# Gate and up as Strassen's seven block products, and a feed-forward in two phases

## The reference, cut to what matters

```python
x = _layernorm(ALPHA * x + g1 * o, ln1_g, ln1_b)
h = x * (1 + sc2) + sh2
gate, up = jnp.split(h @ w_gu, 2, axis=-1)      # 2048 -> 2 x 5632
f = (jax.nn.silu(gate) * up) @ w_down           # 5632 -> 2048
return _layernorm(ALPHA * x + g2 * f, ln2_g, ln2_b)
```

## Time and profile before

| what | value |
|---|---|
| runs, median (lowest, highest) | 3320.02 us (3313.26, 3322.87), 3 runs |
| span of the profiled execution | 3311.0 us |
| its own time beside the span | not given; the median of the runs is 9.0 us above the span |
| PE busy | 3168.8 us, 96% |
| DVE, ACT, POOL busy | 1653.1, 934.4, 207.6 us |
| moved by DMA | 341.86 MB, 103 GB/s |

### The profile page before, as it was taken

How to read it: one execution, slowest core, us unless ns; L and a number is a source line. 1 busy time by engine, 2 the same in 40 slices (tenths; PEclk the granted TensorE clock), 3 DMA queues, 4 the chain that set the end, 5 groups by cost and what they waited for, 6 DMA issues and landing times.

```text
span 3311.0 us, 44092 instructions
## 1 busy us (share of the span) xinstructions
PE 3168.8 (96%) x17294; PEld 2681.6 (81%) x17294; DVE 1653.1 (50%) x2086; ACT 934.4 (28%) x1393; POOL 207.6 (6%) x195
## 2 busy tenths in 40 slices
PE   7899999999999999899999999999999999999994
PEld 2687767777766678698989898989898999999983
DVE  7626665633333332556454535364545454545457
ACT  7425555533444311421211111111111111111121
POOL 0200010100000100062000000000000000000004
PEclk9999999999999999899999999999999999999997
DMA  9836655621200311132222222222222222222221
GB/s 369 275 126 206 196 192 190 206 93 52 108 32 32 123 65 64 45 91 82 71 77 71 77 77 77 74 73 77 72 76 77 77 72 76 77 71 77 77 96 64
DMA packets 91913, 341.86 MB, mean 103 GB/s; under 512 B 11878, under 2 KB 12090, under 8 KB 90714
## 3 DMA queue, kind: packets, MB, share of 16 engines
q1 hardware_dynamic: 82800, 302.55, 27.2%
q0 software_dynamic: 8224, 36.50, 3.4%
q10 hardware_dynamic: 730, 0.38, 0.0%
HBM read 327.42 MB, written 15.65 MB: 104 GB/s over the span
## 4 chain that ended last, share of the span: by engine, by line
PE 83%; DVE 8%; issue 3%; DMA 3%; ACT 2%; POOL 0%; DVEq 0%; ACTq 0%; SPq 0%; POOLq 0%
PE ps L1294 25%; PE ps L1296 25%; PE ps L1295 25%; PE ps L1465 2%; DVE wlo L927 1%; ACT whi L559 1%; DMA mraw<-in_wstream 1%; DVE acc L1278 1%; PE ps L1417 1%; DMA raw<-in_wstream 1%; PE ps L1416 1%; PE ps L1438 1%; DVE tmp L1245 1%; DVE mlo L942 1%; PE ps L1412 1%
## 5 line engine op out<-in xcount | busy, mean ns | idle before, releaser
L927 DVE TENSOR_TENSOR wlo<-raw,whi 128x1024 fp32r<-128x1024 f32 x497 | 617.2, 1249 | 1270.1 <-ACT whi L559 1265.1
L559 ACT ACTIVATE whi<-raw 128x1024 fp32r<-128x1024 f32 x497 | 519.3, 1058 | 1625.9 <-PE ps L1296 1602.5
L1294 PE MATMUL ps<-oh,whi 128*128 128x320 f32 x2816 | 872.3, 310 | 8.7 <-DVE tmp L1245 7.8
L1295 PE MATMUL ps<-ol,whi 128*128 128x320 f32 x2816 | 870.2, 309 | 0.0
L1296 PE MATMUL ps<-oh,wlo 128*128 128x320 f32 x2816 | 870.1, 309 | 0.0
L1294 PEld LDWEIGHTS ps<-oh,whi 128*128 128x128 f32 x2816 | 530.2, 188 | 12.5 <-DVE tmp L1245 11.2
L1295 PEld LDWEIGHTS ps<-ol,whi 128*128 128x128 f32 x2816 | 530.2, 188 | 0.1
L1296 PEld LDWEIGHTS ps<-oh,wlo 128*128 128x128 f32 x2816 | 530.0, 188 | 0.0
L1296 PE MATMUL ps<-whi,fl 128*128 128x512 f32 x820 | 327.0, 399 | 0.0
L1294 PE MATMUL ps<-whi,fh 128*128 128x512 f32 x820 | 322.4, 393 | 4.3 <-DVE wlo L927 3.7
L1295 PE MATMUL ps<-wlo,fh 128*128 128x512 f32 x820 | 323.2, 394 | 0.0
(11 more groups left out here) (251 smaller groups left out, 3831.0 us busy)
## 6 DMA issues: line engine op xcount, KB each, us to landing
raw<-in_wstream SPq DMA_DIRECT2D x503, 512.0 KB, 3.3
mraw<-in_wstream SPq DMA_DIRECT2D x64, 512.0 KB, 7.6
acc<-in_xT SPq DMA_DIRECT2D x8, 640.0 KB, 16.4
oscr<-ost POOLq DMA_DIRECT2D x16, 320.0 KB, 2.4
acc<-in_xtok POOLq DMA_DIRECT2D x1, 5120.0 KB, 16.3
ostage<-oscr POOLq DMA_DIRECT2D x16, 320.0 KB, 4.0
out_y<-acc POOLq DMA_DIRECT2D x5, 1024.0 KB, 4.2
tbl<-rpbpad POOLq DMA_DIRECT2D x16, 224.0 KB, 15.2
```

Source lines behind the costliest of these rows:

```text
L559: nc.scalar.activation(hi_of(n), raw[:, n % 4, :], ACT.Copy).then_inc(hi_ready, 1)
L927: V.tensor_tensor(lo_of(n), raw[:, n % 4, :], hi_of(n).bitcast(f32), ALU.subtract).then_inc(lo_ready, 1)
L1294: mm(out, ah, bh, start=first, stop=False)
L1295: mm(out, ah, bl, start=False, stop=False)
```

## The change

Gate and up are taken as one product of 2 x 2 blocks: the token halves (320 each), the halves of the contraction (1024 each), and gate and up (128 columns each per pair j, 44 pairs). Strassen's scheme (in Winograd's form) needs seven block products in place of eight, and sums of blocks before and after.

**Activations.** The token tiles are transposed in pairs of column tiles kk and kk+8 (`turn_pair`), all 8 pairs before the first product. ScalarE applies scale and shift into a double stage `astage`; GpSimd makes four sums per kk (`sstage`); the seven left factors are kept as high and low parts, `acth` and `actl`. They take the space of the former weight buffers and of oh and ol. The residual `acc` is stored to DRAM (`x1scr`) once LayerNorm is done, since the weight ring and the stages lie in its space, and it is loaded back after the last gate and up product; GpSimd's update with ln1 follows then.

**Weights.** A pair's four blocks fill the four slots of `raw`. VectorE makes four sums of 128 x 1024 per pair (`gu_sum`: zb, xb, yb, yb again); each of the 14 half factors (`HALF`, 128 x 512) is split into a ring of four. GU_BANK puts the seven products on four PSUM banks; ScalarE copies partial results out and VectorE adds them. SiLU is one ScalarE function (`ACT.Silu`) in place of exp, add, reciprocal and multiply. f goes to DRAM (`fscr`) pair by pair. Pairs 0 to 3 are written out; the rest is a loop of two pairs a turn, 20 turns.

**Down.** A phase of its own behind all pairs, with no loop: f comes back in 22 tiles p of 256 columns, and is split again. The weight blocks run in three groups of p (7, 7 and 6 tiles) times four column blocks, 80 blocks, each group accumulating in PSUM and evacuated once; the last two tiles (8 blocks) form the last part as before. The second gate's broadcasts come behind down blocks 2 to 5.

Core of the diff (lines of "..." mark what is left out). SP and GpSimd first:

```diff
+            def gu_load(i, jj):
+                for q in range(4):
...
+                    elif q == 0:
+                        sp.wait_ge(t_ready, at(i, 16, 4 * jj - 2))
+                    elif q == 2:
+                        sp.wait_ge(glo, at(i, 4 * HALF, HALF * (jj - 1) + 12))
+                    row = B_FF + 4 * jj + q
+                    sp.dma_start(raw[:, q, :], wstream[row if i is None else i * GROUP + row]).then_inc(gu_in[q], 16)
...
+            def fk_load(p):
...
+                if p == 2:
+                    sp.wait_ge(f_out[0], 16 * NJ // 2)
+                    sp.wait_ge(f_out[1], 16 * NJ // 2)
...
+            pool.wait_ge(xn_ready, TT)
+            pool.dma_start(x1scr, acc[:, :]).then_inc(x1_out, 16)
+            for kk in range(8):
...
+                pool.wait_ge(a_staged, kk + 1)
+                if kk:
+                    pool.wait_ge(sx_ready, kk)
+                nc.gpsimd.tensor_tensor(sstage[:, 0, :], a21, a[:, 3 * HT:4 * HT], ALU.add)
+                nc.gpsimd.tensor_tensor(sstage[:, 1, :], a11, a21, ALU.subtract).then_inc(s_odd, 1)
+                if kk:
+                    pool.wait_ge(sy_ready, kk)
...
+                nc.gpsimd.tensor_tensor(sstage[:, 2, :], sstage[:, 0, :], a11, ALU.subtract).then_inc(s_two, 1)
+                nc.gpsimd.tensor_tensor(sstage[:, 3, :], a12, sstage[:, 2, :], ALU.subtract).then_inc(s_even, 1)
...
+            pool.wait_ge(gused, HALF * NJ)
+            pool.wait_ge(x1_out, 16)
+            pool.dma_start(selt2[:, :], sel).then_inc(rowsb_in, 16)
+            rows_in(rowsb, D, 5 * D, rowsb_in)
+            pool.dma_start(acc[:, :], x1scr).then_inc(x1_in, 16)
```

ScalarE's list:

```diff
+            a_part(0)
+            a_part(1)
+            for kk in range(8):
+                s_part(kk)
+                if kk + 2 < 8:
+                    a_part(kk + 2)
...
+            def gu_body(i, j):
+                for h in range(HALF):
+                    gu_hi(i, j, h)
+                    if h == 1 and (i is not None or j):
+                        gate0(i, j - 1)
+                    if h == 4 and (i is not None or j):
+                        gate1(i, j - 1)
+                    if h in (5, 7, 9):
...
+                        nc.scalar.activation(ev[:, e, :], ps[bank][:, 0:HT], ACT.Copy)
```

VectorE's list:

```diff
+            a_part(0)
+            for kk in range(8):
+                s_part(kk, 1, sx_hi, sx_ready)
+                if kk + 1 < 8:
+                    a_part(kk + 1)
+                s_part(kk, 3, sy_hi, sy_ready)
...
+                gu_sum(i, j, 0)
+                for h in range(HALF):
+                    if h in (2, 4, 8):
+                        gu_sum(i, j, {2: 1, 4: 2, 8: 3}[h])
+                    gu_lo(i, j, h)
```

TensorE's list, and the broadcasts that move:

```diff
+            def gu_body(i, j):
+                for h in range(HALF):
+                    u, half = divmod(h, 2)
+                    s = (HALF * j + h) % 4
+                    pe.wait_ge(glo, at(i, 2 * HALF, HALF * j + h + 1))
...
+                    out = ps[GU_BANK[u]][:, 0:HT]
+                    for k in range(4):
...
+                        mm(out, ringh[:, s, w], ah, start=first, stop=False, skip_group_check=True)
+                        mm(out, ringh[:, s, w], al, start=False, stop=False, skip_group_check=True)
+                        ins = mm(out, ringl[:, s, w], ah, start=False, stop=last, skip_group_check=True)
+                    ins.then_inc(gused, 1)
+            for j in range(4):
+                gu_body(None, j)
+            with pe.Fori(2, NJ // 2) as i:
+                gu_body(i, 0)
+                gu_body(i, 1)
...
+            for d in range(N_DOWN):
...
+                if d in (2, 3, 4, 5):
...
+                    for c in range(2):
+                        ins = mm(ps[1 + c][:, :], selt2[:, 2 + c * P:2 + (c + 1) * P], rowsb[0:5, q * 512:(q + 1) * 512],
+                                 start=True, stop=True)
-                if b in (26, 28, 30):
-                    pe.wait_ge(rows2_in, 96)
-                    pe.wait_ge(g_evac, b - 18)
-                    gate_bcast(rows2, (b - 26) // 2)
```

More of the change, by code:

```diff
@@ L878, in _ @@
[L878 to L902, removed]
@@ new lines, in gu_hi @@
+            def gu_hi(i, j, h):
+                u, half = divmod(h, 2)
+                H = lambda c: at(i, 2 * HALF, HALF * j + c)
+                if u in (1, 2, 3, 6):
+                    act.wait_ge(t_ready, at(i, 8, 4 * j + {1: 1, 2: 2, 3: 3, 6: 4}[u]))
+                else:
+                    act.wait_ge(gu_in[half if u == 0 else 2 + half], at(i, 32, 16 * (j + 1)))
+                if i is None and j == 0 and h == 0:
+                    act.wait_ge(xt_ready, 8)
+                    act.wait_ge(x1_out, 16)
+                if i is not None or j or h >= 4:
+                    act.wait_ge(gused, H(h - 3))
+                nc.scalar.activation(ring(ringh, (HALF * j + h) % 4), gu_source(u, half), ACT.Copy).then_inc(ghi, 1)
@@ new lines, in _ @@
+            fk_split(0)
+            d_split(0)
+            gate0(None, NJ - 1)
+            d_split(1)
+            fk_split(1)
+            gate1(None, NJ - 1)
+            for d in range(N_DOWN):
+                if d + 2 < 7:
+                    fk_split(d + 2)
+                for n in d_next(d):
+                    d_split(n)
+                if d in (2, 3, 4, 5):
+                    gate2_copy(d - 2)
+                c, p = DOWN[d]
+                if c == 3 and p < 13:
+                    fk_split(p + 7)
+                if (c, p) == (2, 14):
+                    fk_split(20)
+                if (c, p) == (2, 15):
+                    fk_split(21)
@@ L1251, in _, with a_part @@
-            ff_group(None, 0)
-            with dve.Fori(1, NG - 1) as i:
-                own.enter(i, 1, GT * 2 + 4 * TT)
-                ff_group(i, 0)
-                own.leave(NG - 2)
-            ff_group(None, NG - 1, last=True)
-            for n in range(B_LAST + 2, N_BLOCKS):
-                split(None, 0, n)
+            def a_part(kk):
+                a = astage[kk % 2]
+                cols = slice(kk * HT, (kk + 1) * HT)
+                two = a[:, 2 * HT:4 * HT].rearrange("p (s t) -> p s t", s=2)
+                dve.wait_ge(a_staged, kk + 1)
+                V.tensor_copy(acth[:, 0, cols], a[:, 0:HT])
+                V.tensor_copy(acth[:, 5:7, cols], two).then_inc(a_hi, 1)
+                dve.wait_ge(a_hi, kk + 1)
+                V.tensor_tensor(actl[:, 0, cols], a[:, 0:HT], acth[:, 0, cols].bitcast(f32), ALU.subtract)
+                V.tensor_tensor(actl[:, 5:7, cols], two, acth[:, 5:7, cols].bitcast(f32), ALU.subtract).then_inc(a_ready, 1)
@@ L1262, in gain @@
+            d_split(N_DOWN + 7)
             def gain(t):
@@ L1751, in last_part, with down_part @@
+            for j in range(4):
+                gu_body(None, j)
+            with pe.Fori(2, NJ // 2) as i:
+                gu_body(i, 0)
+                gu_body(i, 1)
+            def down_part(m, d, p, t, first, last):
+                hi, lo = dw(d)
+                f = fslot(p)
                 o = slice(t * P, (t + 1) * P)
```

655 lines of the change are left out of this document (444 added, 211 removed).

## The result

| | before | after |
|---|---|---|
| runs, median (lowest, highest) | 3321.44 us (3313.26, 3329.19), 4 runs | 3229.41 us (3226.36, 3242.46), 4 runs |
| span of the profiled execution | 3311.0 us | 3240.9 us |
| PE busy | 3168.8 us, 96% | 3026.0 us, 93% |
| DVE, ACT, POOL busy | 1653.1, 934.4, 207.6 us | 1722.2, 1179.7, 265.1 us |
| moved by DMA | 341.86 MB | 380.00 MB |

The ratio is 0.973, 95% interval 0.9707 to 0.9752: the change makes the kernel 92 us faster. The forecast was 3230.

The account below looks back on a forecast made before the run. TensorE's matmul slots bound the kernel: 1651.2 us of slots plus 64, 2.5, 23.7, 11, 9 and 4 make 1765.4 instead of 1847.8; with the earlier start -89.9, so 3230 us, range 3190 to 3285.

Parts of the forecast that it names:

- The slots of 320: Gate and up: 168 matmuls per pair instead of 192 at 0.1467 us, saving 154.9 us, TensorE 1084.2 instead of 1239.1.
- VectorE and ScalarE can feed it: Per pair of 24.6 us on TensorE, VectorE needs 18.0 and ScalarE 10.6 us, so nothing is added.
- late slots of `raw`: Rival: slots 2 and 3 refilled late, each pair losing 4.1 us, 180 in all, 3410 us; chance 0.07.
- a starved ring: Rival: VectorE's in-order list starves the ring of split halves; at 1 us a pair 3274 us; chance 0.12.
- The ramp: Before the first gate/up product: serial rounds of 7.7 us, 64 us without a product, about 70 by the port rule.
- The jumps: Loop of pairs: 19 jumps back at 1.25 us each, +23.7 us (bounds 10 to 38).
- Down's slots: Down projection: keeps all its matmuls, 2430 slots of 512 columns at 0.2333 us, 567.0 us.
- The passage: Gate/up to down: f tile 2 and weight block 2 land late behind the residual's 5 MB load, +11 us.
- The group changes: Changes of tile group in down: no TensorE wait expected from the evacuations, 0 us charged.
- Gate broadcasts: The four second-gate broadcast calls return in the down phase at 2.2 us each, +9 us (up to 15).
- entry: Entry into the last part: starts 18 us after block 78 where its matmuls would allow 14, +4 us.

Follow-up runs that it names:

- before written out: The kernel before with TensorE's feed-forward loop written out, no jump left, same work: 3316.51 against 3325.20 us, ratio 0.9976.

## Why the prediction was right, and where it was not

- **The slots of 320, right.** 44 x 168 at 0.1467 us, and the eighth product brings back 155.2 us for the 154.9 saved.
- **VectorE and ScalarE can feed it, right.** No wait in 44 pairs; the slower rivals (late slots of `raw`, a starved ring) did not come about.
- **The ramp, right in size and mechanism.** 65.0 for 64, rounds of 7.58 for 7.7. The prediction named the wait for `sy_ready`; taking it away gives 10 us. The Trainium skill's rule on the shared port ("SBUF — State Buffer", "Who interferes with whom") would by the prediction's estimate have made the ramp some 70 us. The trace agrees that the two hinder each other: VectorE's two differences take 1.17 us longer a round, between the one sum of 0.9 that the prediction charged and the nearly two of that estimate. An engine that waits only for the rest of the other's instruction would show this too, so the runs do not decide about the rule.
- **The jumps, wrong: +23.7 became 0.** The failed step is "I read it as 1.25 us for a jump back", carried over to a loop with a third of the body. The gap was rightly the jump's and not the evacuation's (before written out), but it comes only with the longer bodies, which the branch's own duration tells: 4967 ns at 1008 matmuls against 208 at 336.
- **Down's slots, mis-sized: 567.0 became 550.8.** The price was carried over from one pair of tiles to another. Before's own last part runs at 0.2267 with two other weight tiles, which the prediction did not look at.
- **The passage, mis-sized: 11 became about 22.** The mechanism was the one named, tile 2 and block 2 behind the residual. But the prediction had the last f ready 2 us behind the products and both landed near 20 us. The store was issued at 7.7, behind VectorE's split of block 1, and block 2 was there only at 30.5: some five of these ten us are the late issue of the reload, the other five block 2's 19.9 us from issue to use in place of about 15.
- **The group changes, missing: +19.3.** The prediction looked at VectorE's evacuations in down and not at SP's list, where `fk_load` with its wait stands ahead of the weight loads.
- **Gate broadcasts and entry, near.** 10 for 9, 6.5 for 4.

Jumps and slots, 40 us too high together, stand against passage and group changes, 30 too low. The mechanism that carries the result was right. That the saving came within 3 us (89.9 forecast, 92.7 by the stretches) is luck: the misses cancelled.

## What to carry to other kernels

A reload that waits, put on an in-order queue ahead of loads that don't, takes their lookahead away: count what stands behind every wait on the queue, also where the engine's own work looks light. In the same way, ask what an engine's list puts ahead of the last result of a phase: here a split that waits for a transfer held back the store that the next phase reads. A large transfer that nothing needs for long can go in pieces, each ahead of its use, and not whole at a moment when small ones are wanted. And before a gap is priced as "one jump", look at the branch's own duration and the length of the body: with 336 and 672 matmuls a turn it was free here, with 1008 and 1344 it cost 1.2 us each.

## What was not expected of the hardware

- A jump back over 1008 or 1344 matmuls takes TensorE's sequencer 5.0 or 3.5 us, of which 1.2 show; over 336 or 672 matmuls 0.21 us, of which nothing shows.
- The same multiplication of 512 columns takes a slot of 0.2267 or 0.2333 us, depending on which tiles it reads, and moving them by 32, 1032 or 4072 bytes changed it by 0.001 at most (the blocks of 30 matmuls stayed at 7.00, 6.97 and 6.80 us).
- 239 us less work of VectorE beside a busy TensorE are worth 0.6 us, inside the interval.
